# Turning the next pass's rows behind the down projection in a routed mixture-of-experts stage

## The reference, cut to what matters

```
hg = jnp.einsum('td,edf->tef', h, w_gate_e)
hu = jnp.einsum('td,edf->tef', h, w_up_e)
act = jax.nn.silu(hg) * hu * gates[..., None]
routed = jnp.einsum('tef,efd->td', act, w_down_e)
shared = (jax.nn.silu(h @ w_gate_sh) * (h @ w_up_sh)) @ w_down_sh
return routed + shared
```

## Time and profile before

| | |
|---|---|
| median of 3 runs | 1099.96 us (1099.4 to 1100.63) |
| the profiled execution, its own time | 1099.3 us |
| its span in the profile | 1097.5 us |
| PE busy | 934.3 us (85%) |
| DVE busy | 404.1 us (37%) |
| ACT busy | 202.2 us (18%) |
| POOL busy | 242.0 us (22%) |
| mean granted TensorE clock, share of full | 0.946 |

### The profile page before, as it was taken

One profiled execution on the slowest core, in us unless ns is written; L12 is line 12 of the kernel. 1 busy time (PEld: TensorE's weight loads), 2 busy tenths in 40 slices (PEclk: granted clock), 3 DMA queues, 4 the chain that ended last, 5 costly groups with the idle time before them and its releaser, 6 DMA issues.

```text
span 1097.5 us, 13692 instructions
## 1 busy us (share of the span) xinstructions
PE 934.3 (85%) x4773; PEld 440.3 (40%) x4773; DVE 404.1 (37%) x975; ACT 202.2 (18%) x415; POOL 242.0 (22%) x301
## 2 busy tenths in 40 slices
PE   4979987997988889799899897899797979999784
PEld 3564555465534544333333332333232324333231
DVE  5957447857873652123111111111111111111116
ACT  6050031141213131111111110111110111111103
POOL 1910029002300166102111211112111210222012
PEclk9989998998999899899899998999898999999988
DMA  9720120231226118899999999999999999999945
GB/s 325 304 77 5 74 78 0 77 90 70 47 79 231 46 55 346 359 377 385 394 381 384 385 389 392 376 381 374 370 394 382 372 374 376 359 339 388 381 147 195
DMA packets 66421, 289.66 MB, mean 264 GB/s; under 512 B 17291, under 2 KB 18539, under 8 KB 41392
## 3 DMA queue, kind: packets, MB, share of 16 engines
q1 hardware_dynamic: 45376, 250.21, 57.7%
q0 software_dynamic: 13232, 35.04, 12.2%
q10 hardware_dynamic: 7744, 3.53, 1.2%
HBM read 257.14 MB, written 41.18 MB: 272 GB/s over the span
## 4 chain that ended last, share of the span: by engine, by line
PE 47%; issue 29%; DVE 13%; ACT 5%; DMA 4%; ACTq 1%; SPq 0%; POOL 0%; DVEq 0%; POOLq 0%
PE bank L998 24%; PE bank L1944 21%; DVE arena L1592 3%; DVE arena L698 2%; PE bank L1036 2%; DMA prm<-expert_lists 1%; DVE arena L800 1%; ACT arena L1265 1%; DMA sum_rows<-arena,xs 1%; ACT arena L1252 1%; DVE bb L720 1%; DMA qkv_samples<-arena 1%; DVE arena L1923 1%; DMA arena<-in_x_prompt 1%; DVE arena L1905 1%
## 5 line engine op out<-in xcount | busy, mean ns | idle before, releaser
L998 PE MATMUL bank<-arena 128*32 128x512 f32 (+6 forms) x2930 | 539.7, 601 | 82.2 <-issue 52.9
L998 PEld LDWEIGHTS bank<-arena 128*32 128x32 f32 (+3 forms) x2930 | 198.3, 132 | 391.1 <-issue 376.4
L1944 PE MATMUL bank<-arena 128*128 128x512 f32 (+9 forms) x1208 | 309.2, 444 | 32.7 <-ACT arena L1549 8.5
L1944 PEld LDWEIGHTS bank<-arena 128*128 128x128 f32 (+4 forms) x1208 | 173.0, 191 | 162.3 <-issue 128.8
L465 POOL DMA_INDIRECT arena<-h_rows,xs x42 | 43.6, 1039 | 466.7 <-DVE bb L720 455.3
L698 DVE SCALAR_TENSOR_TENSOR arena<-arena,xs,bank 128x256 f32<-128x256 f32 x42 | 27.7, 660 | 312.1 <-issue 271.5
L695 DVE COPY arena<-bank 128x512 f32<-128x512 f32 x41 | 28.4, 692 | 179.1 <-PE bank L998 174.6
L554 ACT ACTIVATE arena<-bank 128x256 f32<-128x256 f32 x42 | 16.1, 383 | 328.7 <-PE bank L998 284.2
L474 POOL DMA_INDIRECT sum_rows<-arena,xs x41 | 64.6, 1576 | 53.4 <-DVE arena L695 30.6
L1592 DVE TENSOR_TENSOR arena<-arena 64x512 f32<-64x512 f32 (+8 forms) x79 | 68.3, 865 | 6.5 <-DMA arena<-o_samples 3.8
L484 POOL DMA_INDIRECT expert_lists<-arena,ncim x40 | 39.8, 994 | 91.4 <-issue 87.7
(11 more groups left out here) (231 smaller groups left out, 529.1 us busy)
## 6 DMA issues: line engine op xcount, KB each, us to landing
arena<-in_w_gate_e SPq DMA_DIRECT2D x64, 1024.0 KB, 18.4
arena<-in_w_up_e SPq DMA_DIRECT2D x64, 1024.0 KB, 34.5
arena<-in_w_down_e SPq DMA_DIRECT2D x64, 1024.0 KB, 33.8
arena<-in_w_in SPq DMA_DIRECT2D x5, 2048.0 KB, 9.0
expert_lists<-arena SPq DMA_DIRECT2D x1, 8482.5 KB, 28.9
arena<-in_x_prompt SPq DMA_DIRECT2D x8, 512.0 KB, 5.9
arena<-in_w_out SPq DMA_DIRECT2D x2, 2048.0 KB, 8.3
arena<-sum_rows SPq DMA_DIRECT2D x8, 512.0 KB, 7.9
```

The costliest lines, as they stand in the source:

```text
L998: return nc.tensor.matmul(o, l, r, start=start, stop=stop, skip_group_check=True)
L1944: return nc.tensor.matmul(o, l, r, start=start, stop=stop, skip_group_check=True, **kw)
```

## The change

The rows of the next pass are turned, and copied, behind the down projection instead of ahead of the two transposes. The same instructions are issued, in another order on PE, ACT and DVE.

```diff
@@ act_unit (ACT)
             nc.scalar.activation(sil[u % 2], bank[(2, 6)[u % 2]][:, 0:FE], ACT.Silu).then_inc(s("silu_done"), 1)
-            if u + 1 < NU:
-                act_rows(act, u + 1)
             act_turn(act, u)
             if u < NU - 1:
                 act_down(act, u)
+            if u + 1 < NU:
+                act_rows(act, u + 1)
             if u + LISTS < NU:
                 act_list(act, u + LISTS)
@@ dve_unit (DVE)
             gated(u % 2, gate[:, u % IDX:u % IDX + 1], bank[(2, 6)[u % 2]]).then_inc(s("act_done"), 1)
+            if u < NU - 1:
+                dve_down(dve, u)
             if u + 1 < NU:
                 dve_rows(dve, u + 1)
-            if u < NU - 1:
-                dve_down(dve, u)
@@ moe_pe (PE)
                 pe_up(pe, u)
                 if u == 4:
                     pe_jobs(pe)
+                pe_act(pe, u)
+                pe_down(pe, u)
                 if u + 1 < NU:
                     pe_rows(pe, u + 1)
-                pe_act(pe, u)
-                pe_down(pe, u)
```

## The result

The changed kernel takes 1170.06 us (median of four runs, 1159.87 to 1174.14) against 1099.68 us before: 1.063 times as long, 95% interval 1.056 to 1.070. That is outside the predicted range, and twice the predicted rise. The profiled execution took 1168.09 us.

The account below looks back on a forecast made before the run. PE and weight loading were taken as two close limits of the routed stage. Added steps 85.5 - weights 59.0 + clock 8 = 34.5 us on 1099.3 gave 1133.8, stated as 1133 us; range 1112 to 1165.

Parts of the forecast that it names:

- the clock: PE's emptied first gap may drop the clock to 1.2 GHz, 1.69 us a fall; 5 falls chosen, 8 us.
- Rival (A): The clock falls in most passes: 18 to 41 falls, 30 to 69 us, giving 1156 to 1195 us; chance 0.14.
- The Trainium skill's rule: Brief waits between matmul groups make the clock go up and down; all 41 passes lose time, 95.5 us instead of 34.5.
- the row: Profile row of the kernel before: a 1.85 us empty wait with transposes ahead of it, the clock staying at 1.00.
- theory 2: Follow-up run's theory: one fall brings the next, so filling every other first gap leaves 4 to 8 falls, 1131 to 1138 us.
- The first half of the pass: From up to down projection, removing the row transposes gains 0, at most 0.05 us, since DVE's product releases PE.
- Rival (C): Row transposes do hold the product's two transposes, so the first half shortens by up to 1.09 us: at best 1081; chance 0.05.
- The added steps: Between down and next up projection, passes 1 to 41 pay 2.21, 2.03 or 1.92 us: 85.5 us.
- The weights: Ten up projections' waits for weights, 39.6 us, and their slow matmuls, 19.4 us, all go: -59.0 us.
- (B): Up projections still wait for weights; at least 15 of the 59.0 us stay: 1149 up to 1185 us; chance 0.11.
- (D): Weights pace the stage so firmly that added PE time only fills waits; time stays within 0.2%; chance 0.02.
- The copies of the down projection: On ACT and DVE, 0.59 and 0.69 us, they run beside the 1.12 us of row transposes and cost nothing.

Follow-up runs that it names:

- Experiment 8: Changed kernel with eight identity transposes between up projection and product transposes in odd passes alone: 1137.31 us, 1.036 of before.
- experiment 1: Changed kernel with eight identity transposes filling the first gap, between up projection and product transposes, in every pass: 1124.44 us, 1.023 of before.
- experiment 4: Kernel before with down blocks loaded for the first six experts alone, later passes reusing them: 1041.45 us, 0.949 of before.
- experiment 5: Changed kernel with down blocks loaded for the first six experts alone, later passes reusing them: 1169.62 us.
- experiment 3: Changed kernel with PE turning rows in the first gap as before, ACT and DVE still copying them behind the down projection's copies: 1107.78 us, 1.009 of before.
- experiment 7: Changed kernel with half the rows turned, and copied by ACT, in the first gap; the other half and DVE's copy behind the down projection: 1110.63 us.
- experiment 6: Changed kernel with four identity transposes, in place of eight, filling the first gap of every pass: 1124.02 us.
- experiment 9: Kernel before with sixteen identity transposes ahead of each of the ten up projections that waited for weights: 1097.89 us, 0.9997 of before.

## Why the prediction was wrong

**The step that failed is the clock.** The prediction chose 5 falls, between bounds of none and 41, and 8 us. The profile after has 28 beside that of pass 4, and 48.7 us of slow down projections in all. The price was right (1.69 us predicted, 5.35 - 3.65 = 1.70 measured); the number was not. With the measured 48.7 in place of the 8, the sum is 1133.8 - 8 + 48.7 = 1174.5, against 1168.09 for the profiled execution. Of the 6.4 us between them, 2.7 are the slow matmuls around pass 4 in the kernel before, which the prediction left out, and some 3 lie outside the routed stage: the stage grew by 72.1 us, the execution by 68.8. Rival (A), with 18 to 41 falls and 1156 to 1195 us, is what happened. The Trainium skill's rule that was set against the row (TensorE: Matmul & The Clock Gate, A second HAM failure mode) came nearer than the row: the trace after agrees with it in 28 of 41 passes, and not in the other 13.

Two things were wrong in how the number was chosen. First, one row without a fall (1.85 us empty) was read as a safe side, which left only the 18 passes with 32 rows in doubt. After the change 14 of those 18 fell (pass 4 among them), but also 10 of the 15 passes with 64 rows and 5 of the 9 with 128, which had 1.22 + 0.51 = 1.73 us empty in the pass shown above. A single instance of an event that comes in some cases and not in others bounds nothing. The trace of the kernel before had nearer rows, in pass 4 and in the last pass, which the prediction does not use:

```profile
526.36 1.09 PE L1015 MATMUL bank<-ident,arena 128*128 128x128 f32 x8
528.89 0.63 PE L1036 MATMUL bank<-ident,arena 128*128 128x128 f32 x2 [1.44 <-DVE arena L698]
530.29 13.23 PE L998 MATMUL bank<-arena 128*32 128x512 f32 x96 [0.77 <-ACT arena L534]
...
1070.98 0.44 PE L1036 MATMUL bank<-ident,arena 128*128 128x128 f32 x2 [1.17 <-DVE arena L698]
1072.06 3.65 PE L998 MATMUL bank<-arena 128*64 128x512 f32 x16 [0.65 <-issue]
```

In pass 4 the product came late, and the granted clock was 0.50 from 529.0 us on, behind only 1.44 us empty with the eight transposes just ahead: 1.85 us was no safe side. The last pass has no next rows to turn, so its first gap was already the one that the change makes everywhere, and its clock stayed at 1.00. The trace before thus had a fall below the safe side, and one such gap without a fall, which leaves the whole range open. Second, falls were counted as separate events. Experiment 8 speaks against that: with every other gap filled, 6 of 20 fell instead of some 14. That a pass made longer by a fall meets the same conditions in the next pass fits the 17.07 us intervals, and was predicted by theory 2 with 4 to 8 falls; how the chip decides is not shown by these runs.

**What held.** The first half of the pass gained nothing: L1036 starts 1.22 us after the up projection, released by L698 (experiment 1 shows it from the other side, where eight transposes come back at no cost). Rival (C) is out. The added steps sum to 85.0 us against 85.5, though not by kind: the prediction had 2.21, 2.03 and 1.92 us for 32, 64 and 128 rows, and they are 2.08, 2.06 and 2.08 on average, so that the close sum is in part luck. The weights gave back some 59 us: shown by experiment 4 (59.3 us of stage with less traffic), by experiment 5 (no effect of the same cut after the change) and by experiment 1, whose 1124.4 us is the sum without falls, 1099.3 + 26.5 = 1125.8. Rivals (B) and (D) are out: no up projection waits beyond the copies. The copies of the down projection were hidden beside the row transposes, and no L1015 waited for a gather. In experiments 3 and 7 part of that cover is lost, and both of DVE's copies stand on PE's path, one behind the other.

So the 70.4 us between the medians are some 25 us for turning and copying the rows on PE's path, net of the weights, and some 46 us for the clock: experiment 1 takes out 45.6 us (1170.06 - 1124.44) with instructions that compute nothing.

## What to carry to other kernels

Before moving PE work out of a wait that seems to hide it, ask what PE will then do in that wait: here the work was free in time, and it kept the clock up for the matmuls behind it. Time on PE's path can be paid out of waits for weights as long as these last, so sum those first, with the slow matmuls that follow them, and compare. Where a cost comes as an event that may or may not happen in each pass, take the range from "none" to "every pass" and look for a reason why one makes the next more likely, before trusting a few rows. Search the whole trace of before for waits of the same shape: here pass 4 and the last pass had them.

## What the runs showed of the hardware

The lower clock level followed a first gap of about 1.2 us empty, 0.44 us of two transposes and 0.5 to 0.8 us empty, in 28 of 41 passes; it did not follow 1.58 to 1.60 us that were wholly empty between a down and an up projection (experiment 3), nor the same first gap with 0.66 us of transposes more (experiment 6). The length of the empty time alone does not decide: in the kernel before 1.44 us (pass 4) and 1.99 us were followed by the lower level, while in experiment 9 a wait of 2.27 us without transposes (748.37) was not. Transposes of the identity, with no other use, kept the level at 2.4 GHz.

The slow stretches are regular: 17.07 us apart in 22 of 28 intervals in the changed kernel, 92.16 us apart six passes on with every other gap filled. The four runs of the changed kernel differ by 1.2% and those of experiment 8 by 0.1%; over the former the mean granted clock goes with the time, from 0.937 at 1159.87 us to 0.927 at 1174.14 us.
